# A one-core backbone step: spreading the second gate and the final norm by TensorE, moving a branch, and loading the last down weights in four pieces

## What is computed

```python
def moe_ffn(x, w_router, router_bias, w_gate, w_up, w_down):
    ...
    gates = jnp.sum(jax.nn.one_hot(idx, N_EXPERTS, dtype=jnp.float32) * w[..., None], axis=1)
    h = jax.nn.silu(jnp.einsum("td,edf->tef", t, w_gate)) * jnp.einsum("td,edf->tef", t, w_up)
    h = h * gates.astype(h.dtype)[..., None]
    return jnp.einsum("tef,efd->td", h, w_down).reshape(B, L, D)

def trunk_layer(P, l, x, cond, rg_h0, hg_s0, ret_s0, lb, rope):
    mod = jnp.dot(jax.nn.silu(cond), P["w_ada"][l]) + P["b_ada"][l]
    sh1, sc1, g1, sh2, sc2, g2 = jnp.split(mod[:, None, :], N_MOD, axis=-1)
    ...
    x = x + g2 * moe_ffn(h, P["w_router"], P["router_bias"], P["w_gate"][l], P["w_up"][l], P["w_down"][l])
    return x, st_rg, st_hg, st_ret
...
y_prompt = rmsnorm(xc, norm_final)
y_sample = rmsnorm(xs, norm_final)
```

## Time and profile before

| | us |
|---|---|
| median of three runs | 637.57 |
| lowest and highest of them | 637.26 and 640.65 |
| the profiled execution, its own time | 638.13 |
| its span, first to last instruction | 636.3 |
| mean granted clock of PE | 0.971 |
| PE busy | 559.2 |
| PEld busy | 377.2 |
| DVE busy | 245.8 |
| ACT busy | 138.7 |
| POOL busy | 67.1 |

### The profile page before, as it was taken

The page is one execution under the profiler, slowest core; times in us unless marked ns, Lnnn a source line. Parts: engine busy times, 40 slices in busy tenths (PEclk is TensorE's granted clock), DMA queues, the critical chain, the costliest instruction groups (busy, mean ns, idle before and its releaser), DMA issues.

```text
span 636.3 us, 13128 instructions
## 1 busy us (share of the span) xinstructions
PE 559.2 (88%) x5700; PEld 377.2 (59%) x5700; DVE 245.8 (39%) x533; ACT 138.7 (22%) x265; POOL 67.1 (11%) x99
## 2 busy tenths in 40 slices
PE   1799999999999899869998899999999866778674
PEld 0475553566675655765456789998876534445331
DVE  2562457986855754541056841110111000001135
ACT  1241543423216720100026010101111000000013
POOL 2029100000004000002001010100100000100131
PEclk9989999999999999979999999999999999989968
DMA  8989930123030570899939989999999999999962
GB/s 258 392 296 372 368 125 25 58 75 133 1 132 10 178 287 1 301 329 285 363 137 363 396 265 401 397 406 406 402 408 405 405 404 409 409 410 409 330 218 101
DMA packets 80140, 176.06 MB, mean 277 GB/s; under 512 B 6504, under 2 KB 11631, under 8 KB 79695
## 3 DMA queue, kind: packets, MB, share of 16 engines
q1 hardware_dynamic: 65808, 149.08, 62.9%
q0 software_dynamic: 5920, 18.36, 8.0%
q10 hardware_dynamic: 8351, 7.73, 3.8%
HBM read 162.68 MB, written 12.47 MB: 275 GB/s over the span
## 4 chain that ended last, share of the span: by engine, by line
PE 33%; SPq 9%; DMA 8%; DVE 4%; issue 2%; ACT 0%; DVEq 0%
PE psum L937 10%; PE psum L929 5%; PE psum L827 5%; DMA slot<-in_w_down 4%; PE psum L926 4%; SPq L1161 4%; DMA slot<-in_w_gate 3%; PE psum L834 2%; SPq L1174 1%; SPq L1190 1%; PE psum L843 1%; PE psum L487 1%; PE psum L1106 1%; SPq L1178 1%; SPq L1231 1%
## 5 line engine op out<-in xcount | busy, mean ns | idle before, releaser
L575 PE MATMUL psum<-hT,slot 128*128 128x384 f32 x304 | 100.8, 489 | 0.0
L937 PE MATMUL psum<-slot,xeTa 128*32 128x256 f32 x1152 | 67.9, 387 | 14.4 <-DMA slot<-in_w_gate 7.3
L575 PEld LDWEIGHTS psum<-hT,slot 128*128 128x128 f32 x304 | 56.9, 190 | 38.2
L937 PEld LDWEIGHTS psum<-slot,xeTa 128*32 128x32 f32 x1152 | 44.5, 112 | 36.3 <-issue 11.6
L584 PE MATMUL psum<-slot,hT 128*128 128x512 f32 x96 | 42.3, 595 | 1.1 <-DMA slot<-in_w_in 1.1
L937 PE MATMUL psum<-slot,heT 128*32 128x256 f32 x576 | 35.5, 399 | 7.8 <-DMA slot<-in_w_down 7.3
L1690 ACT ACTIVATE he<-psum 128x256 f32<-128x256 f32 (+1 forms) x16 | 6.6, 411 | 135.8 <-PE psum L937 106.5
L2381 DVE COPY heT<-psum 128x256 f32<-128x256 f32 (+1 forms) x16 | 7.3, 458 | 70.0 <-PE psum L956 70.0
L2377 DVE TENSOR_TENSOR he<-he,psum 128x256 f32<-128x256 f32 (+1 forms) x16 | 7.3, 455 | 67.8 <-PE psum L937 49.4
L926 PE MATMUL psum<-slot,xeTa 128*32 128x384 f32 x288 | 32.9, 487 | 0.3 <-issue 0.3
L1365 POOL DMA_INDIRECT xe<-h_rows,lst x15 | 14.3, 951 | 178.2 <-PE psum L946 123.3
(11 more groups left out here) (479 smaller groups left out, 917.0 us busy)
## 6 DMA issues: line engine op xcount, KB each, us to landing
slot<-in_w_ada SPq DMA_DIRECT2D x12, 2048.0 KB, 13.2
slot<-in_w_gate SPq DMA_DIRECT2D x12, 2048.0 KB, 18.1
slot<-in_w_up SPq DMA_DIRECT2D x12, 2048.0 KB, 18.4
slot<-in_w_down SPq DMA_DIRECT2D x12, 2048.0 KB, 18.2
slot<-in_w_in SPq DMA_DIRECT2D x7, 2048.0 KB, 13.6
const<-in_w_gate SPq DMA_DIRECT2D x4, 1792.0 KB
y_rows<-T POOLq DMA_DIRECT2D x11, 384.0 KB, 15.1
slot<-in_w_out SPq DMA_DIRECT2D x2, 2048.0 KB, 15.6
```

Of the source, the lines that this page charges most:

```text
L575: last = mm(o[:, 0:TOK], w[:, kt, tile(i)], hT[:, kt, :], start=(kt == 0), stop=(kt == KT - 1))
L937: last = mm(psum[32 * c:32 * c + 32, bank, 0:HALF], x(k, c % 2), w(k)[:, c // 2 * HALF:c // 2 * HALF + HALF], start=(k == 0), stop=(k == t ...
```

## The change

Three things change.

1. **The second gate and the norm's gain come from PE.** `gate_rows_out` for rows 10 and 11, the three broadcasts and ACT's broadcast of `norm_final` are gone. A load of 4 KB puts `norm_final` as eight rows of 128 into `VR` (POOL, behind the loads of `XR`). `spread_rows(i)` multiplies a column of the identity, repeated 128 times, by the rows, which puts the row on all partitions: four products of 128 x 128 into bank 1 or 7. It is called twice in each of the positions 11, 12 and 13, between the transposes and down. ACT copies each result out of PSUM (six copies of 512 columns), into `G2` (now in the buffer `GX`) or `NF` (now in a part of `const` that is no longer used). DVE makes `G2P` from `G2` by eight copies of 64 x 256.
2. **The branch on the further passes moves** on PE, DVE, ACT and POOL: from after position 15 (on ACT and POOL from after or among the final steps) to between positions 14 and 15 (on PE and DVE), and before the final gather (on ACT and POOL). The passes then use the other set of buffers, and the second gather is gone.
3. **The last down.** SP loads w_down of position 15 in four pieces of 512 KB, each with its own count. PE carries the residual of tile 2 before the last down, once `heT` is ready, and does the last down by pieces (`down_by_pieces`), each behind the count of its piece.

The diff, cut to its core:

```diff
-        G2 = slot[home(0, 2)][:, 0:4, :].rearrange("p (c k) n -> p c (k n)", c=2)
+        G2 = GX[:, :, :].rearrange("p (c h) n -> p c (h n)", c=2)
...
-        NF = ye[1]
+        spread_over = const[:, cols["dft_ctx"][0]:cols["dft_ctx"][0] + 2 * D]
+        NF = spread_over[:, D:2 * D]
...
+                if n in (11, 12, 13):
+                    spread_rows(2 * n - 22)
+                    spread_rows(2 * n - 21)
+                if n == E - 1:
+                    pe.wait_ge(s["ht_ready"], E)
+                    carry(2, 0)
+                    carry(2, 1)
+                if n == E - 1:
+                    pe.wait_ge(s["ya"], n)
+                    pe.wait_ge(s["yb"], n)
+                    down_by_pieces().then_inc(s["down_done"], 1)
+                    return
...
+            def down_by_pieces():
+
+                w = weights(E - 1, 2)
+                for k in range(FE // P):
+                    if k > 0:
+                        name, count = (("third_gate", 32), ("third_up", 48), ("third_down", 80))[k - 1]
+                        pe.wait_ge(s[name], count * (use(11) + 1) + 16)
+                    for half in range(2):
+                        for c in range(4):
+                            a0 = k // 2 * SMALL + c % 2 * 32
+                            last = mm(psum[32 * c:32 * c + 32, 5 + half, 0:HALF], heT[:, k % 2, a0:a0 + 32],
+                                      w[k][half][:, c // 2 * HALF:c // 2 * HALF + HALF], start=(k == 0),
+                                      stop=(k == FE // P - 1), tile_position=(0, 32 * c))
+                return last
+
+            def spread_rows(i):
+
+                if i >= 2:
+                    pe.wait_ge(s["g2_out"], i - 1)
+                c, h = i // 2, i % 2
+                if i == 4:
+                    pe.wait_ge(s["nf_in"], 16)
+                for g in range(4):
+                    n, r = (P, 32 * g + c) if i < 4 else (32, 4 * h + g)
+                    last = mm(psum[:, (1, 7)[i % 2], tile(g)], ident[0:n, r:r + 1].to_broadcast([n, P]),
+                              modrow[:, h, :] if i < 4 else VR[0:n, :], start=(g == 0), stop=(g == 3), skip_group_check=True)
+                last.then_inc(s["spread"], 1)
...
             more = further(pe)
             expert(E - 2)
-            expert(E - 1)
...
             with pe.If(more > 0):
...
-                pe.wait_ge(s["o_z"], 1)
-                for j in range(2):
-                    for h in range(2):
-                        carry(j, h)
-
-            for h in range(2):
-                carry(2, h)
+                pe.wait_ge(s["o_y"], OVER)
+                pe.wait_ge(s["o_lst"], OVER)
+                for h in range(2):
+                    carry(0, h)
+
+            expert(E - 1)
...
+            sp.wait_ge(s["down_done"], user_before(E - 1) + 1)
+            for k in range(FE // P):
+                dst = slot[home(1, 2)][:, 2 * k:2 * k + 2, :].rearrange("p k n -> p (k n)")
+                sp.dma_start(dst, A["w_down"][0, bass.ds(e, 1)].rearrange("o (k p) d -> p (o k) d", p=P)[:, k, :]
+                             ).then_inc(loaded[home(1, 2)] if k == 0 else s[("third_gate", "third_up", "third_down")[k - 1]], 16)
...
+            pool.dma_start(VR[0:KT, :], A["norm_final"].rearrange("(r n) -> r n", n=P)).then_inc(s["nf_in"], 16)
...
-            gate_rows_out(1, 10)
-            gate_rows_out(1, 11)
-            for i in range(2, 4):
-                pool.wait_ge(s[f"gate_w{i}"], 32)
-            pool.wait_ge(s["down_done"], E - 1)
-            pool.dma_start(G2[:, :, :], A["gate_rows"][1:2].to_broadcast([P, 2, D])).then_inc(s["g2_in"], 16)
-            for q in range(2):
-                pool.dma_start(G2P[q * SMALL:q * SMALL + SMALL].rearrange("p c h n -> p (c h) n"),
-                               A["gate_rows"][1:2].rearrange("o c (h q n) -> o (c h) q n", h=2, q=2)[:, :, q, :]
-                               .to_broadcast([SMALL, 4, HALF])).then_inc(s["g2_in"], 16)
...
+                    if n in (11, 12, 13):
+                        for i in (2 * n - 22, 2 * n - 21):
+                            act.wait_ge(s["spread"], i + 1)
+                            to = G2[:, i // 2, i % 2 * CW:i % 2 * CW + CW] if n < 13 else NF[:, i % 2 * CW:i % 2 * CW + CW]
+                            a(to, psum[:, (1, 7)[i % 2], :], ACT.Copy).then_inc(s["g2_out"], 1)
...
-            act.dma_start(NF[:, :], A["norm_final"].rearrange("(o n) -> o n", o=1).to_broadcast([P, D])
-                          ).then_inc(s["nf_in"], 16)
...
+                    if n in (11, 12):
+                        for i in (2 * n - 22, 2 * n - 21):
+                            dve.wait_ge(s["g2_out"], i + 1)
+                            for q in range(2):
+                                r = slice(q * SMALL, q * SMALL + SMALL)
+                                a0 = i % 2 * CW + q * HALF
+                                last = v.tensor_copy(G2P[r, i // 2, i % 2, :], G2[r, i // 2, a0:a0 + HALF])
+                            last.then_inc(s["g2p_out"], 1)
```

More of the change, by code:

```diff
@@ L1051, in _ @@
             pe.wait_ge(s["sel"], NT + 3)
+            pe.wait_ge(s["g2_out"], 6)
             for j in range(NT):
@@ L1740, in _ @@
                     act.wait_ge(s["o_out"], 32 * o + 32)
+            for j in range(NT):
+                act.wait_ge(s[f"fin_in{j}"], 32)
+                a(YG[0][:, j, :], YG[0][:, j, :], ACT.Copy, scale=gw[:, j, 0:1]).then_inc(s["fin_w"], 1)
             for j in range(NT):
@@ L2369, in experts @@
                     n = 2 * it + p
+                    if last_pair and p == 1:
+                        with dve.If(more > 0):
+                            further_rows()
                     if halves and p == 0:
@@ L2398, in _, with further_rows @@
             v.tensor_copy(SELT, psum[:, 7, 0:TOK]).then_inc(s["lists"], 1)
-            more = further(dve)
-            experts(E // 2 - 1, False, True)
-            def gated(j):
-                link(v.scalar_tensor_tensor(YG[0][:, j, :], YG[1][:, j, :], gw[:, j, 1:2], YG[0][:, j, :],
-                                            ALU.mult, ALU.add))
-                return v.tensor_tensor(YG[0][:, j, :], YG[0][:, j, :], G2[:, min(j, 1), :], ALU.mult)
-            dve.wait_ge(s["g2_in"], 48)
-            dve.wait_ge(s["down_done"], E)
-            for c in range(2):
-                v.tensor_tensor(Y15[c], psum[:, 5:7, 0:HALF], G2P[:, c], ALU.mult).then_inc(s["y15"], 1)
-            for j in range(NT):
-                dve.wait_ge(s["fin_w"], j + 1)
-                gated(j).then_inc(s["zed"], 1)
-            with dve.If(more > 0):
+            def further_rows():
                 link_further = steps(dve, "o_step")
-                dve.wait_ge(s["up_done"], E)
+                dve.wait_ge(s["up_done"], E - 1)
                 for o in range(OVER):
@@ L2435, in _, with gated @@
                     v.tensor_copy(yp[0], psum[:, 5:7, 0:PACK]).then_inc(s["o_y"], 1)
-                dve.wait_ge(s["o_fin"], 32 * NT)
-                for j in range(NT):
-                    link_further(v.tensor_scalar(YG[0][:, j, :], YG[0][:, j, :], gw[:, j, 0:1], None, ALU.mult))
-                    link_further(v.scalar_tensor_tensor(YG[0][:, j, :], YG[1][:, j, :], gw[:, j, 1:2], YG[0][:, j, :],
-                                                        ALU.mult, ALU.add))
-                    last = v.tensor_tensor(YG[0][:, j, :], YG[0][:, j, :], G2[:, min(j, 1), :], ALU.mult)
-                last.then_inc(s["o_z"], 1)
+            more = further(dve)
+            experts(E // 2 - 1, False, True)
+            def gated(j):
+                link(v.scalar_tensor_tensor(YG[0][:, j, :], YG[1][:, j, :], gw[:, j, 1:2], YG[0][:, j, :],
+                                            ALU.mult, ALU.add))
+                return v.tensor_tensor(YG[0][:, j, :], YG[0][:, j, :], G2[:, min(j, 1), :], ALU.mult)
+            dve.wait_ge(s["g2p_out"], 4)
+            dve.wait_ge(s["down_done"], E)
+            for c in range(2):
+                v.tensor_tensor(Y15[c], psum[:, 5:7, 0:HALF], G2P[:, c], ALU.mult).then_inc(s["y15"], 1)
+            dve.wait_ge(s["g2_out"], 6)
+            for j in range(NT):
+                dve.wait_ge(s["fin_w"], j + 1)
+                gated(j).then_inc(s["zed"], 1)
             def final_var(j):
```

62 lines of the change are left out of this document (28 added, 34 removed).

## The result

Over six runs each, the changed kernel took 634.53 us (632.95 to 636.97) against 637.41 us (636.85 to 640.65) before: a ratio of 0.9942, 95% interval 0.9915 to 0.9968. The forecast was 634.0 (632.0 to 636.8). The profiled execution has a span of 632.7 us (636.3 before) and a time of 634.58 (638.13): -3.6 us. The total is right; the path to it is not.

A forecast was written before the change was run, and what follows sets the result against it. Two tied chains, PE's through the late w_down of 15 and the gather's, were taken as the bound. The gather's 3.9 us gain less 0.3 gave -3.6 us: 637.57 to 634.0 us, range 632.0 to 636.8.

The forecast's parts named there:

- Step 1: Positions 11 to 13: PE's spreads cost up to +1.9 us, gate of 14 may regain 1.7; +0.3 us taken.
- Rival A: Spreads not covered: lower clock at 568 us stays, position 13's whole 1.9 us counts; -2.0 us, 635.6; chance 0.22.
- Step 2: Without broadcasts w_down of 15 lands by 598 to 600; PE's 4.60 us wait goes, pieces bring nothing, rows take 6.4 us.
- Step 3: PE's 2.97 us stop moves unchanged behind down of 14, whose count is seen at 596.8; PE goes on at 597.1.
- Step 4: PE behind the stop: 12.8 us plus 1.8 for the clock; down of 15 ends at 611.7, Y15 at 613.0.
- Step 5: Gather starts at 603.8 instead of 607.70; DVE leaves the last tile at 621.5 instead of 625.35, 3.9 us earlier.
- the later chain by a little: The gather's chain, forecast 3.9 us earlier against 4.3 us for PE's chain, so it would set the end.
- the sign that I had named for a wrong forecast: DVE still waits for down_done of 15 when the first gathered tile is scaled, and the last tile is then late.
- Rival C: PE's chain sets the end, by 3.5 us of lower clock with the whole +1.9, or a second stop; 636.6; chance 0.12.
- Rival B: The stop costs nothing at its new place, or the count isn't held: gather about 602.3, -5.4 us, 632.2; chance 0.10.

The follow-up runs named there:

- doubled spread: Changed kernel with the spreading products of position 13 written twice (eight more products of 128 columns): 640.92 us, ratio 1.006.
- Part 1 alone: Kernel before with gates and gain spread by PE instead of broadcasts; branch and last down as before: 631.06 us, ratio 0.9906.
- parts 2 and 3: Changed kernel with the second gate and final norm sent again as DMA broadcasts, no spreading: 639.1 us, ratio 1.0028.
- early branch: Changed kernel with PE's branch between positions 9 and 10 and everything behind it written twice on PE: 629.99 us, ratio 0.9873.
- one load: Changed kernel with w_down of 15 in one load and the ordinary down instead of four pieces: 640.48 us, ratio 1.0049.
- both shifted ones: Fifty extra 10x10 transpositions early on PE, in the changed kernel with w_down of 15 in one load and in the changed kernel: 639.85 and 639.51 us.
- parts 1 and 3: Changed kernel with PE's branch and its body moved back behind position 15: 634.07 us, ratio 0.9943.
- short branch: Changed kernel with the body of PE's branch cut to six small products: 632.68 us, ratio 0.9926.

## Why the prediction was right, and where it was not

**Step 1, the spreads.** Right. 2.05 us in position 13, gate of 14 at 3.66 us (the drop of the clock is gone, for 5.35 in the earlier trace rows), down of 14 0.5 us later (590.69 instead of 590.19); +0.3 was taken. Rival A did not happen. The doubled spread shows how near it was: with 2.3 us more of spreading the clock was at 0.77 and 0.66 there.

**Step 2, the broadcasts.** Right in its direction, and it was worth more than it was given. The weights are through at about 602 (the last piece, issued at 588.84, takes 13.1 us to land), not by 598 to 600, and PE needs them at 609.83. Part 1 alone gives 6.2 us, more than all that was forecast. The pieces shortened no wait in the changed kernel, as said. That they bring nothing is not shown: the run without them had a late count, which hides anything smaller than its 5 us. From issue to gather the rows took 7.5 us; 6.4 was taken from a range of 5.7 to 7.4.

**Step 3, the branch.** This is the step that failed, twice. Its size: I carried 2.97 us from the old place to the new; it is 4.78. The branch on PE's sequencer, in ns, in the changed kernel and in the one with the doubled spread:

```profile
L1100 PEldq COMPARE_BRANCH  x1: 6204/6204/6204, 592.9 to 592.9; - x1
...
L1100 PEldq COMPARE_BRANCH  x1: 3620/3620/3620, 599.3 to 599.3; - x1
```

In the six traces where weights were still coming (changed kernel, parts 2 and 3, early branch, one load, both shifted ones) it lasts 6.1 to 6.3 us, and the block is fetched 3.6 to 3.7 us after its start (where two blocks start in that time, in parts 2 and 3 and with the early branch, I take the second). In the five where they were in, or through within 0.4 us (kernel before twice, part 1 alone, parts 1 and 3, doubled spread) it lasts 3.6 to 4.5 us, and the block is fetched 1.6 to 2.1 us after its start in the four with the gather in flight, and 1.1 us in the doubled spread, where the DMA engines were nearly idle (a share of 0.04). The only row for the stop came from a stretch where no weights were on the way, and my term had no upper bound for one where they are. Its effect on the count: I read the 2.67 us of late count as held by the branch, and so put the count of 14 at 596.8. DVE copied it at 594.41, in the 0.1 us that is usual, 4.7 us before PE went on. What holds the count in the kernel before is open (below).

**Step 4, PE's chain.** Behind the stop the working holds: 12.8 us plus 1.8 for the clock were set, 14.4 came (599.12 to 613.49; the carry 3.19 for 1.98, up 4.09 for 3.66). Down of 15 ends at 613.5 instead of 611.7, which is the stop's error.

**Step 5, the gather's chain.** First gather at 602.38 instead of 603.8: 2.4 us earlier since nothing held the count, 1.1 later since the rows took 7.5 us. The third scaling followed it by 12.2 us, not by the 13.92 of the trace before, and came at 614.61, 3.1 us before its forecast. So PE's chain was 1.9 us later (Y15 ends at 614.92, not 613.0), by the stop's size; the gather's chain was 3.1 us earlier, by the count and by a faster gather; and what I called "the later chain by a little" was the earlier one by 4 us. This is the sign that I had named for a wrong forecast: DVE still waits for down_done of 15 (until 613.54) when the first gathered tile is scaled (610.27), and the last tile is then late.

That the total came out so near is luck: the errors moved two chains in opposite directions, and the later of them ended where the other had been forecast. DVE's last tile was forecast for 621.5 by the gather's chain and ends at 622.27 by PE's: 3.1 us before the 625.35 of the kernel before, where 3.9 were forecast. The last output goes out 3.1 us earlier as well (ACT issues it at 627.35 instead of 630.42 us), and the other 0.5 us of the 3.6 lie behind that issue, where the prediction had nothing change. Rival C had the right chain at the end, for reasons that did not come (a longer spell of the lower clock with the whole of the 1.9 us, or a second stop) and at a higher price. Rival B had half of it (the count is not held, gather at 602.3) and for the other half the contrary of what happened.

**What the parts are worth**, from medians: part 1 alone -6.2 us; parts 1 and 3 -3.1; the whole -2.9 beside its own runs of before; parts 2 and 3 without 1, +1.9. The loss of 3 us against part 1 alone stands out of the scatter (five of its six runs are at 629.89 to 632.39 us, all six of the whole at 632.95 to 636.97), but part 1 alone ran on chip 15 and the whole on one that is not on record. How it divides is not settled. Without the branch, or with it early, the change reaches 630 on chip 15, so the stop at a place without cover costs some 4.5 us where it stands, as the traces show it; with a near target it was 632.7 on chip 2. With the branch behind position 15, the stop behind the last down and the gaps in down take nearly as much. That the two causes do not add, since either alone would put PE's chain behind the gather's, is argued and not tested.

**Open: the late counts and gaps.** They have one thing in common. In all nine traces that show one (the kernel before twice, the two shifted ones, one load, doubled spread, parts 2 and 3, parts 1 and 3, short branch) it falls 3 to 9 us behind the first issue of the gather, while its transfers are in flight; elsewhere in these traces, under loads at 400 GB/s too, the counts of products came within 0.1 us of their modelled ends (one gap, of 0.28 us, stands 1.0 us ahead of the gather, in parts 2 and 3). But not everything in that window is hit: in the changed kernel up of 15 ends 4.0 us behind the first issue, and its count comes 0.05 us later; with no branch, or an early one, down of 15 ends 5.0 and 5.6 us behind it, without harm.

A second thing goes with them, and no run separates it: the chip. All eight traces that were taken on chip 2 show a late count or gaps, and none of the four from chip 15 does; of the two whose chip is not on record, the kernel before shows one and the changed kernel none. That the kernel before takes the same time on both chips does not settle it, for its end hardly depends on the count of down of 15: Y15 is done at 614.87, before the first gathered tile is scaled, at 615.74. So what makes PE's products or their counts late there, and whether it is the place of the instructions, the timing against the gather or the chip that switches it on, is open. It was not tried to run one kernel on both chips with a trace of each, to delay the gather, or to take it by another queue.

## What to carry to other kernels

Before a stop is moved, ask what covers it where it stands, and size it from a trace of the load at its new place, not of the old: the same far branch took 3.6 to 4.5 us on PE's sequencer with the weights in and 6.1 to 6.3 with them coming. If a branch must be, put it where the loads set the pace. Test each part of a change alone: here the first part alone gave 6 us and the whole gave 3, which the sum hides, and a forecast near the sum with it. And before a difference of 0.5% between two edited kernels is believed, run both on the same chip.

## What was not expected of the hardware

- A far taken branch on PE waits for a 16 KB block in the instruction queue: 2.2 to 3.0 us of idle with the weights in and work of PE's queued ahead of it (3.6 us in parts 1 and 3), 4.7 to 4.9 and once 5.9 us with them coming, none with a near target. PE goes on 2.4 to 2.8 us after the block's transfer starts; what varies is the time before that.
- Counts of PE's products came 2.3 to 5.3 us after their modelled ends while an indirect gather was in flight, in six of the traces, and down of 15 had gaps of 0.3 to 0.8 us between its products in three more. The cause is open, the chip among the candidates.
